# ScalarE's copy of unfinished sums before the next pair's high part, three units side by side at the joints, and an earlier third low half

## The reference

```python
for i in range(DEPTH):                       # 2
    h = modulate(x, norm_g[i, 0], shift, scale)
    x = x + 0.5 * gate * swiglu(h, ffn_w13[i, 0], ffn_w2[i, 0])
    h = modulate(x, norm_g[i, 1], shift, scale)
    y = mlstm_mixer(h, ...) if i % 2 == 0 else diff_attn_mixer(h, ...)
    x = x + gate * y
    h = modulate(x, norm_g[i, 2], shift, scale)
    x = x + 0.5 * gate * swiglu(h, ffn_w13[i, 1], ffn_w2[i, 1])
return rmsnorm(x, final_g)

def swiglu(h, w13, w2):
    gate, up = jnp.split(h @ w13, 2, axis=-1)      # inner width 2816
    return (jax.nn.silu(gate) * up) @ w2
```

## Time and profile before

| | |
|---|---|
| median of 3 runs | 1932.04 us (1931.3 to 1932.08) |
| profiled execution | 1932.38 us, of which the span of instructions is 1930.6 us |
| mean granted TensorE clock | 0.995 of full speed |
| TensorE busy | 1893.5 us |
| VectorE busy | 1417.1 us |
| ScalarE busy | 894.8 us |
| DMA | 273.51 MB, mean 142 GB/s |

### The profile page before, as it was taken

The page is one execution under the profiler, slowest core; times in us unless marked ns, Lnnn a source line. Parts: engine busy times, 40 slices in busy tenths (PEclk is TensorE's granted clock), DMA queues, the critical chain, the costliest instruction groups (busy, mean ns, idle before and its releaser), DMA issues.

```text
span 1930.6 us, 30347 instructions
## 1 busy us (share of the span) xinstructions
PE 1893.5 (98%) x11816; PEld 1694.8 (88%) x11816; DVE 1417.1 (73%) x2017; ACT 894.8 (46%) x1418; POOL 18.7 (1%) x19
## 2 busy tenths in 40 slices
PE   7999999999999999999999999999999999999998
PEld 5799998888679899998899999889877799999887
DVE  6778878685566788878768888796786768888433
ACT  7356642244244566652255666223444446666321
POOL 3000000000000000000000000000000000000000
PEclk9999999999999999999999999999999999999999
DMA  8733359524112423249733232972321233223432
GB/s 318 286 107 109 109 204 340 207 90 151 55 55 83 146 90 109 109 152 338 271 121 121 88 108 82 340 254 88 105 70 44 67 122 118 93 103 104 134 96 80
DMA packets 85970, 273.51 MB, mean 142 GB/s; under 512 B 8528, under 2 KB 18896, under 8 KB 84856
## 3 DMA queue, kind: packets, MB, share of 16 engines
q1 hardware_dynamic: 85680, 271.83, 41.0%
q10 hardware_dynamic: 200, 0.52, 0.1%
HBM read 261.82 MB, written 10.50 MB: 141 GB/s over the span
## 4 chain that ended last, share of the span: by engine, by line
PE 90%; DVE 5%; DMA 2%; ACT 1%; issue 1%; SPq 0%; DVEq 0%; ACTq 0%
PE acc L676 14%; PE acc L677 13%; PE acc L678 13%; PE outp L676 13%; PE outp L678 12%; PE outp L677 12%; PE stats L678 2%; PE stats L677 2%; PE stats L676 2%; DVE w_lo L1683 1%; PE outp L976 1%; DMA arena<-w 1%; DMA early_ada<-ada 1%; ACT w_hi L1188 1%; PE acc L1072 1%
## 5 line engine op out<-in xcount | busy, mean ns | idle before, releaser
L676 PE MATMUL acc<-h_hi,w_hi 128*128 128x256 f32 (+1 forms) x1220 | 401.5, 329 | 11.3 <-DVE w_lo L1683 5.9
L1188 ACT ACTIVATE w_hi<-arena 128x1024 fp32r<-128x1024 f32 (+2 forms) x231 | 209.9, 909 | 390.0 <-DMA arena<-w 169.4
L677 PE MATMUL acc<-h_lo,w_hi 128*128 128x256 f32 (+1 forms) x1220 | 390.1, 320 | 0.0
L678 PE MATMUL acc<-h_hi,w_lo 128*128 128x256 f32 (+1 forms) x1220 | 389.9, 320 | 0.0
L1896 DVE TENSOR_TENSOR w_lo<-arena,w_hi 128x1024 fp32r<-128x1024 f32 (+1 forms) x272 | 290.5, 1089 | 118.7 <-ACT w_hi L1264 118.7
L1683 DVE TENSOR_TENSOR w_lo<-arena,w_hi 128x1024 fp32r<-128x1024 f32 (+2 forms) x229 | 236.8, 1037 | 180.1 <-ACT w_hi L1188 178.5
L1264 ACT ACTIVATE w_hi<-arena 128x1024 fp32r<-128x1024 f32 (+1 forms) x272 | 258.4, 951 | 197.3 <-DVE arena L1879 143.4
L676 PE MATMUL outp<-g_hi,w_hi 128*128 128x512 f32 (+1 forms) x792 | 290.8, 367 | 0.0
L677 PE MATMUL outp<-g_lo,w_hi 128*128 128x512 f32 (+1 forms) x792 | 289.7, 366 | 0.0
L678 PE MATMUL outp<-g_hi,w_lo 128*128 128x512 f32 (+1 forms) x792 | 289.6, 366 | 0.0
L676 PEld LDWEIGHTS acc<-h_hi,w_hi 128*128 128x128 f32 x1220 | 233.1, 191 | 37.6 <-issue 6.8
(11 more groups left out here) (281 smaller groups left out, 3413.6 us busy)
## 6 DMA issues: line engine op xcount, KB each, us to landing
arena<-w SPq DMA_DIRECT2D x174, 512.0 KB, 3.8
ada_raw<-ada SPq DMA_DIRECT2D x64, 512.0 KB, 5.6
arena<-ada SPq DMA_DIRECT2D x56, 512.0 KB, 5.6
arena<-w SPq DMA_DIRECT2D x64, 384.0 KB, 3.4
arena<-w SPq DMA_DIRECT2D x64, 320.0 KB, 3.7
arena<-wa SPq DMA_DIRECT2D x33, 512.0 KB, 3.5
arena<-wb SPq DMA_DIRECT2D x32, 512.0 KB, 3.6
early_ada<-ada SPq DMA_DIRECT2D x8, 1024.0 KB, 17.4
```

Source lines behind the costliest of these rows:

```text
L676: pe.matmul(bank, a_hi, b_hi, start=start, stop=False, skip_group_check=onto)
L677: pe.matmul(bank, a_hi, b_lo, start=False, stop=False, skip_group_check=onto)
L678: return pe.matmul(bank, a_lo, b_hi, start=False, stop=stop, skip_group_check=onto)
L1188: act.activation(w_hi[base % SLOTS][:, 0:n], src[:, 0:n], ACT.Copy).then_inc(hi_ready, 1)
```

## The change

Three places in the orders of three engines. TensorE: in the second half of the tokens, `first_group` takes units U, U + 1 and U + 2 side by side, and only U + 3 afterwards. ScalarE: in a fast pair `tap(j, 1)` comes before `factor_high(j + 1, 0)`. VectorE: in a joint `low_part(U + 2)` comes before the last residual and its addition (after a network), or before the last addition (after a mixer). Nothing is computed that was not computed before, and no instruction is added or removed.

```diff
@@ first_group (TensorE)
                 for half in range(2):
+                    together = 3 if half else 2
                     for k in range(KT):
                         pe.wait_ge(act_lo_ready, Q_IN[n] + 8 * half + k + 1)
-                        for s in range(2):
+                        for s in range(together):
                             if half == 0 and k == 0:
                                 pe.wait_ge(lo_ready, U + s + 1)
                                 take_acc(T, s)
                             product(s, k, half)
-                    for s in range(2, 4):
+                    for s in range(together, 4):
@@ fast_pairs (ScalarE)
                     tap(j, 0)
                     factor_high(j, 3)
+                    tap(j, 1)
                     factor_high(j + 1, 0)
-                    tap(j, 1)
                     if j:
                         fast_high(j - 1)
@@ norm (VectorE)
                 lows(Q_IN[n], ada_v[:, 3 * n, :], lambda k: modulated(k, 0), tok(0))
+                low_part(U + 2)
                 if mixer:
                     add(7)
                 else:
                     update()
-                low_part(U + 2)
-                if not mixer:
                     add()
                 low_part(U + 3)
```

## The result

After the change the median is 1919.72 us (1917.86 to 1922.45, four runs), beside 1932.06 us for the kernel before on the same chip (1931.3 to 1933.11, four runs). The ratio is 0.9937, with a 95% interval of 0.992 to 0.9954: 12.2 us faster by the ratio (12.3 by the medians), where 12.1 were forecast and 1920.0 as the time. The profiled execution took 1919.8 us around a span of 1918.0; the span is 12.6 us shorter.

A forecast was written before the change was run, and what follows sets the result against it. TensorE was taken to bound the kernel, busy 1893.5 of 1930.6 us, with stalls between matmuls not printed as idle. Terms -10.9 - 1.9 + 0.7 = -12.1 us gave a median of 1920.0; own range 1918.3 to 1922.2, wider range 1914.2 to 1923.0.

The forecast's parts named there:

- The ScalarE edit: Fast pairs: copying `tap(j,1)` earlier removes TensorE's stall of 0.16 to 0.17 us in 64 of 68 pairs, -10.9 us.
- the lower bound, 64 x 0.16: Fast pairs: the least gain given for ScalarE's new order, 10.2 us.
- The low half ahead of the residual: Joints: TensorE's wait for the third low half shortens by 0.40 in three and 0.33 in two, -1.9 us.
- The cover for the sum of squares: Joint after a network: the sum, delayed by the low part, is still ready 0.3 us before TensorE asks.
- Three units side by side: Half 1 of five joints: wins 4.7 us, gives back 5.4 as the first unit ends 1.6 later; +0.7 together.
- The other two terms: Second mixer: fourth-bank wait 1.15 us, net +0.3. Network 3: wait 0.95 before the first pair, net +0.1.
- rival 2: Half-clock stretch at 1571.6 to 1575.0 goes: 1918.3; or new waits bring one to each of five joints: 1928.5. Chance 0.12.
- 1: Joints: three units side by side keep their 4.7 us because some slack is larger than read: 1914.5. Chance 0.15.
- 3: Fast pairs: ScalarE's new order gives nothing, TensorE waits for something else ending then; only joints gain: 1930.8. Chance 0.05.
- 4: Fast pairs: `factor_high(j+1,0)` held back too far, costing from 3.6 us on; at 3.8 us +13.6, 1944.4. Chance 0.02.

The follow-up runs named there:

- the version with two products: Kernel after, but in half 1 the third unit's products are put in behind tiles 2 and 4 only: 1915.8 us, ratio 0.9911; on another chip 1915.31, ratio 0.9916.
- the third edit alone: Kernel before with only three units side by side in half 1 on TensorE: 1932.6 us beside 1933.63, ratio 0.9995.
- the first alone: Kernel before with only ScalarE's order changed, `tap(j, 1)` ahead of `factor_high(j + 1, 0)`: 1921.62 us, ratio 0.9932.
- the kernel with four units: Kernel after, with all four units side by side in half 1: 1935.57 us, ratio 1.0017 against the kernel before.
- the copy held back: Kernel after, with `tap(j, 1)` moved ahead of `factor_high(j, 3)` too: 2137.84 us, one run.
- The version with three products: Kernel after, third unit's products behind tiles 1, 3 and 5, second mixer's fourth copy ahead of the waiting high part: 1916.2 us, then 1915.63.

## Why the prediction was right

- **The ScalarE edit** was the gain, by the step that was named: 10.2 us for 10.9. From the first to the last fast pair, network 0 went from 133.37 to 131.28 us, each of the others from 174.30 to 171.60. A regular pair gained 0.154 us (10.234 to 10.080), not 0.17; there are 56 of them. The first two of each network gained about 0.2 each. The 0.17 was taken from single steps rounded to 0.01 us (0.40 for 0.24), and the lower bound, 64 x 0.16, met the measured sum because these two errors cancel. Sixteen pairs measured end to end would have said it.
- **The low half ahead of the residual**: 0.40, 0.34, 0.39, 0.39 and 0.34 us, 1.9 in all, as forecast (0.40 three times, 0.33 twice). The cover for the sum of squares held.
- **Three units side by side** won 0.90 or 0.91 a joint (forecast 0.94) and gave it back. With the slow first steps after a wait, which the forecast had too (0.10), the net was +0.24, +0.14, +0.13, -0.16 and +0.40: +0.75 for +0.7. In the first mixer and in networks 1 and 2 that is the forecast: a new wait of 0.88, 0.77 and about the same again, and the slow steps, for 0.95 and 0.10. The other two terms missed in opposite directions, and that the sum fits is luck. In the second mixer the copy came as late as forecast (the load behind it was issued 0.54 us later from the start of half 1, forecast 0.53), but the load could be used 3.57 us after its issue, 4.09 before, and the wait was 0.63 (from 1350.77 to 1351.40), not 1.15. Nor is the late first unit the only cause there: the version with two products has a wait at that bank without it. In network 3 a load issued for the first pair landed 4.83 us after its issue, 3.29 before, and VectorE waited 0.39 us for it: the wait was 1.04. With this edit alone the load took 3.40 and the net was +0.15; in the second trace of the kernel after it took 5.11 and the net was +0.68. Why the load takes longer there stays open.
- **The later wait in the first mixer** (0.23 us; 0.39 in the second trace) was not in the sum. It is the same late end of the first unit, met once more behind a load.
- **The clock** was not in the sum either: -1.6 us, where half of rival 2 had -1.7 in another place. With it the terms give 10.2 + 1.9 - 0.75 - 0.23 + 1.6 = 12.7, and 12.6 were measured. That the median came out within 0.3 of the forecast is partly luck: the first term was 0.7 too large, the later wait was missing, and the clock gave 1.6.
- **The rivals.** 1 fell with the third edit alone, 3 with the first alone. Of 2, the stretch that it named is still there. 4 was right in kind, as far as the neighbouring high part shows: held back for 2.9 us further it sets the pair's length. Its price was set too low since the clock was left out, and its threshold was not measured.

## What to carry to other kernels

A copy that frees another engine belongs in an in-order stream just ahead of the work that can bear to wait, not one place earlier: here one place won 10 us and the next lost 218. Where a busy engine shows no idle time, take the distance between the same instruction of two successive passes and divide by the number of steps; what is over is a stall, whatever the busy share says. And when gaps are to be filled, put in as much work as the gaps hold: two or three products of the third unit kept 0.7 or 0.9 us a joint, eight gave it back, because the first unit's end starts the next chain. Last, a copy that frees a bank should not stand behind work that waits for a load: both mixers had such a place, and each showed only once TensorE or the load had shifted.

## What the runs showed of the hardware

- A stretch of 3.4 us at the lower clock level (0.50) can follow a wait of TensorE, and the length of the wait alone does not decide. Behind the wait of 1.95 us in the first mixer 4 of the 13 traces have one (the kernel before and three others), the kernel after has none, and the two traces of the version with two products differ. In the kernel with four units the waits of 1.8 to 3.4 us at all five joints had one; with the copy held back, 57 of 64 pairs had one, behind waits of about 1.83 us. Behind a wait of 1.69 us in the first mixer no trace has one. Yet three traces have one in the second mixer behind a wait of 1.01 or 1.02 us, the shortest with one behind it. The version with three products, first trace, TensorE and the sums behind it:

```profile
1432.60 1.05 PE L1110 MATMUL stats<-ones,b_qk 128*128 128x1 f32 x8 [1.02 <-DVE b_qk L2299]
```
```profile
1434.85:1438.25 3.40, 3.40 (x10) 2.62 (x9) 3.26 (x9) 1.92 (x5) 0.00 (x0) 0.50 0.05 19
```

  Behind single waits of 0.6 to 0.99 us there was none between the opening and the last normalisation. What decides stays open.
- This goes with the spread from run to run. In the ten runs of the versions with two and three products in the last series the mean granted clock goes from 0.994 to 0.997; with two products, runs at 0.994 took 1919.5 and 1919.6 us, and those at 0.996 and 0.997 took 1915.0 to 1915.3. With three products the order is less clean (1914.7 and 1917.7 us, both at 0.995). A gain of 1 us can't be seen in such medians.
- A wait costs TensorE more than is printed: the matmul behind the wait of 0.88 us has the next one 0.31 behind it instead of 0.23 (410.71, then 411.02), and the stall of 0.16 us in each fast pair was printed as no idle time at all.
